# Two-layer decoder trunk on one core: expert rows gathered and results added by indirect transfers instead of one-hot products

## The reference, cut to what matters

```python
def moe_swiglu(h, w_router, wg, wu, wd):          # h = rms_norm(x, norm_ffn)
    logits = (h @ w_router).astype(jnp.float32)
    top_v, top_i = lax.top_k(logits, TOP_K)
    gate = jax.nn.softmax(top_v, axis=-1)
    comb = jnp.sum(jax.nn.one_hot(top_i, N_EXPERTS, dtype=jnp.float32) * gate[..., None], axis=-2)
    out = jnp.zeros_like(h)
    for e in range(N_EXPERTS):
        out = out + comb[..., e:e + 1].astype(h.dtype) * swiglu(h, wg[e], wu[e], wd[e])
    return out                                    # x = x + out; then rms_norm(x, norm_final)
```

## Time and profile before

| | us |
|---|---|
| median of 3 runs | 1719.57 (1717.74 to 1722.81) |
| profiled execution, its own time | 1716.31 |
| its span, first to last instruction | 1714.5 |
| PE busy, share of the span | 1655.3, 97% |
| DVE busy, share | 1229.0, 72% |
| ACT busy, share | 1007.0, 59% |
| HBM read | 457.94 MB, 268 GB/s over the span |
| granted clock of TensorE, mean | 0.991 |

### The profile page before, as it was taken

The page is one execution under the profiler, slowest core; times in us unless marked ns, Lnnn a source line. Parts: engine busy times, 40 slices in busy tenths (PEclk is TensorE's granted clock), DMA queues, the critical chain, the costliest instruction groups (busy, mean ns, idle before and its releaser), DMA issues.

```text
span 1714.5 us, 22148 instructions
## 1 busy us (share of the span) xinstructions
PE 1655.3 (97%) x9025; PEld 1405.8 (82%) x9025; DVE 1229.0 (72%) x879; ACT 1007.0 (59%) x835; POOL 17.3 (1%) x26
## 2 busy tenths in 40 slices
PE   7889999999998999899999999999999999999997
PEld 7769889999876987788878888888888788888885
DVE  5646555444664645888888888888888888888884
ACT  6544343434454434576766767667766677667662
POOL 0000000000000001000000000000000000000000
PEclk9989999999999999899999999999999999999999
DMA  8514425555451345699999999999999998999981
GB/s 312 197 50 160 158 84 206 188 188 199 171 206 50 148 148 197 222 368 362 341 348 356 354 356 344 350 362 346 366 353 351 347 361 341 354 367 346 362 338 73
DMA packets 36327, 459.78 MB, mean 268 GB/s; under 512 B 4144, under 2 KB 4400, under 8 KB 6448
## 3 DMA queue, kind: packets, MB, share of 16 engines
q1 hardware_dynamic: 35424, 455.52, 70.5%
q0 software_dynamic: 848, 3.48, 0.6%
HBM read 457.94 MB, written 1.05 MB: 268 GB/s over the span
## 4 chain that ended last, share of the span: by engine, by line
issue 59%; PE 32%; DVE 4%; ACT 3%; DMA 1%; SPq 0%; POOL 0%; DVEq 0%; ACTq 0%; POOLq 0%
PE PS L734 9%; PE PS L736 9%; PE PS L735 9%; DMA stage<-wl_dram 1%; DVE wlo L1263 1%; ACT probs L418 1%; PE PS L1027 1%; PE PS L999 1%; ACT whi L379 1%; PE PS L740 1%; PE PS L771 1%; PE PS L798 1%; PE PS L817 0%; DVE loA L1281 0%; DVE probs L1306 0%
## 5 line engine op out<-in xcount | busy, mean ns | idle before, releaser
L1263 DVE TENSOR_TENSOR wlo<-stage,whi 128x4096 fp32r<-128x4096 f32 (+2 forms) x226 | 926.4, 4100 | 287.3 <-ACT whi L379 286.1
L379 ACT ACTIVATE whi<-stage 128x4096 fp32r<-128x4096 f32 (+2 forms) x227 | 765.1, 3372 | 366.4 <-DMA stage<-wm_dram 231.3
L734 PE MATMUL PS<-whi,e_hi 128*128 128x512 f32 x896 | 357.1, 399 | 5.7 <-DVE wlo L1263 2.8
L736 PE MATMUL PS<-whi,e_lo 128*128 128x512 f32 x896 | 351.7, 392 | 0.0
L735 PE MATMUL PS<-wlo,e_hi 128*128 128x512 f32 x896 | 350.8, 392 | 0.0
L734 PEld LDWEIGHTS PS<-whi,e_hi 128*128 128x128 f32 x896 | 169.5, 189 | 40.3 <-DVE wlo L1263 3.8
L736 PEld LDWEIGHTS PS<-whi,e_lo 128*128 128x128 f32 x896 | 169.2, 189 | 36.1
L735 PEld LDWEIGHTS PS<-wlo,e_hi 128*128 128x128 f32 x896 | 169.6, 189 | 33.3
L734 PE MATMUL PS<-whi,a_hi 128*128 128x512 f32 x448 | 176.2, 393 | 3.4 <-DVE a_lo L1772 2.4
L735 PE MATMUL PS<-wlo,a_hi 128*128 128x512 f32 x448 | 174.7, 390 | 0.0
L736 PE MATMUL PS<-whi,a_lo 128*128 128x512 f32 x448 | 174.6, 390 | 0.0
(11 more groups left out here) (296 smaller groups left out, 1849.7 us busy)
## 6 DMA issues: line engine op xcount, KB each, us to landing
stage<-wm_dram SPq DMA_DIRECT2D x167, 2048.0 KB, 9.4
stage<-wl_dram SPq DMA_DIRECT2D x20, 2048.0 KB, 8.0
stage<-wf_dram SPq DMA_DIRECT2D x33, 1024.0 KB, 4.8
stage<-wl_dram SPq DMA_DIRECT2D x7, 1816.0 KB, 8.8
w1k<-wl_dram SPq DMA_DIRECT2D x2, 2048.0 KB, 7.7
w1v<-wl_dram SPq DMA_DIRECT2D x2, 2048.0 KB, 12.1
xs<-mem_dram POOLq DMA_DIRECT2D x2, 1024.0 KB, 7.9
stage<-wm_dram SPq DMA_DIRECT2D x2, 1024.0 KB, 6.0
```

Of the source, the lines that this page charges most:

```text
L379: nc.scalar.activation(whi[slot][:, 0:n], stage[slot][:, 0:n], ACT.Copy).then_inc(w_hi[slot], 1)
L734: mm(out, ah, bh, start=start, stop=False)
L736: return mm(out, al, bh, start=False, stop=stop)
L1263: V.tensor_tensor(wlo[slot][:, 0:n], stage[slot][:, 0:n], f32(whi[slot][:, 0:n]), ALU.subtract).then_inc(w_lo[slot], 1)
```

## The change

- **Rows in.** POOL writes x once to an HBM tensor `x_rows` (and a second copy to `sums`). For each item from the second on, POOL gathers the 128 rows of the slots from `x_rows` into `xg` by an indirect DMA (`take`), and PE turns them by 8 transposes (`turn_rows`) into the banks in which the gather's products were before. The first item is still gathered by products (`gather`), now from the unscaled x.
- **Norm factor.** x is gathered without its norm factor. The factor of each slot (`rstd_slot`) is the scale of silu (on the gate product) and a scalar operand of the product of silu and up.
- **Slot facts.** One pair of small products per item (`info`) gives row number, whether the slot is used, norm factor and weight of each slot, from `info_tok`. DVE makes of them the row to take and the row to add to (an unused slot adds to a spare row behind the 256).
- **Rows out.** ACT scales the item's sum and writes it in float32 (`rows_of`); there is no split, no scatter product and no scatter add. POOL adds the rows to `sums` in HBM by an indirect DMA with accumulation (`put`).
- **Last item.** It is scattered on chip as before; its one-hot matrix is made and turned again behind the loop. Before that POOL has loaded x back from `sums`.

```diff
@@ gpsimd, behind the layers
+            pool.wait_ge(x_half, 8)
+            pool.dma_start(x_rows.rearrange("(t p) d -> p t d", p=P), x[:]).then_inc(rows_out, 16)
+            pool.dma_start(sums[0:SEQ, :].rearrange("(t p) d -> p t d", p=P), x[:]).then_inc(put_done, 16)
+            def take(it):
+                pool.drain()
+                pool.wait_ge(take_ready, it)
...
+                    pool.wait_ge(gath_done, it * 2)
+                nc.gpsimd.tensor_tensor(pool_step[:], stat[:, 2:3], stat[:, 3:4], ALU.mult)
+                pool.indirect_dma_start(out=xg[:], out_offset=None, in_=x_rows, in_offset=bass.IndirectOffsetOnAxis(ap=take_next[:], axis=0)) \
+                    .then_inc(xg_in, 16)
+            def put(it):
+                pool.drain()
+                pool.wait_ge(dn_ready, it)
+                pool.wait_ge(put_ready, it)
+                pool.wait_ge(put_done, it * 16)
+                nc.gpsimd.tensor_tensor(pool_step[:], stat[:, 2:3], stat[:, 3:4], ALU.mult)
+                pool.indirect_dma_start(out=sums, out_offset=bass.IndirectOffsetOnAxis(ap=put_now[:], axis=0), in_=down_rows[:], in_offset=None,
+                                        compute_op=ALU.add).then_inc(put_done, 16)
+            take(1)
...
+            with pool.Fori(1, n_items) as it:
+                put(it)
+                take(it + 1)
+            pool.drain()
+            pool.wait_ge(put_done, n_items * 16)
+            nc.gpsimd.tensor_tensor(pool_step[:], stat[:, 2:3], stat[:, 3:4], ALU.mult)
+            pool.dma_start(x[:], sums[0:SEQ, :].rearrange("(t p) d -> p t d", p=P)).then_inc(x_back, 16)
@@ scalar
-                act.wait_ge(f_rstd, NT + t + 1)
-                nc.scalar.activation(xs_hi[:, t, :], x[:, t, :], ACT.Copy, scale=stat[:, 6 + t:7 + t]).then_inc(xg_hi, 1)
+                act.wait_ge(x_half, 4 + 2 * t + 2)
+                nc.scalar.activation(xs_hi[:, t, :], x[:, t, :], ACT.Copy).then_inc(xg_hi, 1)
+            def rows_of(it):
+                act.wait_ge(put_ready, it)
+                act.wait_ge(put_done, it * 16)
+                nc.scalar.activation(down_rows[:].rearrange("p (b n) -> p b n", b=2), PS[:, 2:4, :], ACT.Copy, scale=gate_slot).then_inc(dn_ready, 1)
-                        down_parts()
+                        rows_of(it)
-                    nc.scalar.activation(hid_tok[:, 0, :], bank(0), ACT.Silu).then_inc(m_silu, 1)
+                    if s == 0:
+                        act.wait_ge(slot_ready, it + 1)
+                    nc.scalar.activation(hid_tok[:, 0, :], bank(0), ACT.Silu, scale=rstd_slot).then_inc(m_silu, 1)
-                    if s == 5:
-                        act.wait_ge(ohT_done, it + 1)
-                        nc.scalar.activation(gate_slot, bank(6)[:, SEQ:SEQ + 1], ACT.Copy)
-                        nc.scalar.activation(onehot_T[:], bank(6)[:, 0:SEQ], ACT.Copy).then_inc(ohT_ready, 1)
@@ tensor
+            def info(cols):
+                for t in range(NT):
+                    ins = mm(bank(5)[:, cols], f32(onehot[:, t, :]), info_tok[:, t, cols], start=(t == 0), stop=(t == NT - 1))
+                ins.then_inc(info_done, 1)
+            def turn_rows(it):
+                pe.wait_ge(xg_in, it * 16)
+                for k in range(KD):
+                    ins = nc.tensor.transpose(bank(6 + k // 4)[:, (k % 4) * P:(k % 4) * P + P], xg[:, k * P:(k + 1) * P], ident)
+                    if k % 4 == 3:
+                        ins.then_inc(gath_done, 1)
-                        pe.wait_ge(ohT_ready, it + 1)
-                        gather(it + 1)
+                        turn_rows(it + 1)
-                            pe.wait_ge(md_lo, it)
+                            pe.wait_ge(dn_ready, it)
-                    if 1 <= s <= 4 and not first:
-                        scatter(it, s - 1)
-                    if s == 4:
...
+                    if s == 3:
+                        pe.wait_ge(oh_ready, it + 2)
+                        info(slice(0, 4))
@@ vector
-                V.tensor_tensor(hid_tok[:, 1, :], hid_tok[:, 0, :], bank(1), ALU.mult).then_inc(m_mul, 1)
+                V.scalar_tensor_tensor(out=hid_tok[:, 1, :], in0=bank(1), scalar=rstd_slot, in1=hid_tok[:, 0, :],
+                                       op0=ALU.mult, op1=ALU.mult).then_inc(m_mul, 1)
-                    if s == 1 and not first:
-                        down_parts(it)
-                    if 2 <= s <= 5 and not first:
-                        scatter_add(it, s - 2)
+                    if s == 2:
+                        if not first:
+                            dve.wait_ge(put_done, it * 16 + 16)
+                            V.tensor_copy(put_now[:], put_next[:])
+                            V.tensor_copy(gate_slot, info_next[:, 3:4]).then_inc(put_ready, 1)
+                        dve.wait_ge(info_done, it + 2)
+                        onehots(it + 1)
+                        gate_of(it + 1, oh_ready)
+                    if s == 4:
+                        dve.wait_ge(info_done, it + 3)
+                        V.tensor_copy(info_next[:], bank(5)[:, 0:4]).then_inc(row_done, 1)
...
+                        V.tensor_copy(take_next[:], info_next[:, 0:1]).then_inc(take_ready, 1)
```

More of the change, by code:

```diff
@@ L721, in _ @@
                     nc.scalar.activation(a_hi[:], bank(4), ACT.Copy).then_inc(ma_hi, 1)
+            act.wait_ge(ohT_done, 1)
+            nc.scalar.activation(onehot_T[:], bank(5)[:, 0:SEQ], ACT.Copy).then_inc(ohT_ready, 1)
             act.wait_ge(w_used[2], n_items * MOE_STEPS + MOE_USED[2])
+            act.wait_ge(put_ready, n_items)
+            act.wait_ge(put_done, n_items * 16)
             down_parts()
@@ L1211, in item @@
                     if s == MOE_STEPS - 1:
-                        pe.wait_ge(ohT_ready, it + 1)
-                        gather(it + 1)
+                        turn_rows(it + 1)
                     if not begin:
                         if s == 1 and not first:
-                            pe.wait_ge(md_lo, it)
+                            pe.wait_ge(dn_ready, it)
                         down_e(n, s == 1, s == 0)
-                    if 1 <= s <= 4 and not first:
-                        scatter(it, s - 1)
-                    if s == 4:
[L1221 to L1226, removed]
+                    if first and s == 1:
+                        pe.wait_ge(gt_ready, 1)
+                        info(slice(3, 4))
+                    if s == 3:
+                        pe.wait_ge(oh_ready, it + 2)
+                        info(slice(0, 4))
             pe.wait_ge(xg_lo, 2)
             gather(0)
+            pe.wait_ge(info_ready, 1)
+            info(slice(0, 3))
             item(0, first=True)
@@ L1236, in _ @@
             turn(steps)
+            pe.wait_ge(oh_last, 1)
+            for t in range(NT):
+                ins = nc.tensor.transpose(bank(5)[:, t * P:(t + 1) * P], f32(onehot[:, t, :]), ident)
+            ins.then_inc(ohT_done, 1)
             keep_busy(7, 40)
@@ L1697, in onehots, with slots_of, gate_of @@
                     ins = V.tensor_scalar(onehot[:, t, :], cst("iota", 0, CAP), 1.0, keys[:, t, bass.ds(it, 1)], ALU.add, ALU.is_equal)
-                ins.then_inc(oh_ready, 1)
-            def gate_of(it):
-                V.tensor_copy(gate_tok, combs[:, :, bass.ds(it, 1)].rearrange("p t o -> p (t o)")).then_inc(gt_ready, 1)
+                return ins
+            n_row = [0]
+            def slots_of():
+                V.scalar_tensor_tensor(out=row_f[:], in0=info_next[:, 1:2], scalar=spare_neg, in1=info_next[:, 0:1], op0=ALU.mult, op1=ALU.add) \
+                    .then_inc(row_done, 1)
+            def gate_of(it, ready=None):
+                V.tensor_copy(info_tok[:, :, 3:4], combs[:, :, bass.ds(it, 1)]).then_inc(ready or gt_ready, 1)
             def mlo(kind, n):
@@ L1727, in _ @@
             gathered_lo(0)
+            dve.wait_ge(info_done, 1)
+            V.tensor_copy(rstd_slot, bank(5)[:, 2:3]).then_inc(slot_ready, 1)
+            V.tensor_copy(info_next[:, 0:3], bank(5)[:, 0:3]).then_inc(row_done, 1)
+            dve.wait_ge(row_done, 1)
+            slots_of()
+            dve.wait_ge(row_done, 2)
+            V.tensor_scalar(put_now[:], row_f[:], spare, None, ALU.add)
             mlo(0, 1)
```

89 lines of the change are left out of this document (57 added, 32 removed).

## The result

The changed kernel takes 1729.74 us (median of 20 runs, 1721.65 to 1744.04), the kernel before 1722.47 us (20 runs, 1713.84 to 1728.59). The ratio is **1.0048, interval 1.0034 to 1.0063**: slower by some 8 us (6 to 11 by the interval), where 9.0 were forecast. So the two traces are 18.6 us apart where the medians are 7.3 apart. Counts, shapes and the kind of waits can be compared between them; a difference of one or two us per item can't.

What follows compares the result with a forecast made beforehand. PE and the buffers' ring were taken to bind together. PE in items -8, end -2.7, DMA +19.2 and start +0.5 sum to +9.0 us, from 1719.57 to 1728.6 us; likeliest case 1722 to 1738, full range 1707 to 1752.

Steps and rivals of the forecast that it cites:

- Both loops bind together: Expert stage: PE has work for 99.6% of an item, and the buffers' ring runs flat out for 98.8%.
- Forecast A: Expert stage: ring bound, half of the new DMA time reaches it, 1722 to 1738 us; chance 0.40.
- 0.2 us per step: Expert stage: the time a buffer's ring waits for PE, 17.6 us ring against 17.8 step; some 1.5 us per item.
- The term -8 us for PE in the items: Seven items: the ring gives back 1.2 us each of what it waits for PE; bounds 0 and -11 us.
- I take 1.2 us for the items: Per item: two thirds or more of the ring's 1.5 us wait for PE, as some slots are late for DMA.
- the end's 2.7: Last item: its uncovered 3.5 us gather for an item that doesn't exist becomes 0.8 us, saving 2.7 us.
- The term +19.2 us for DMA: Expert stage: half of 38.3 us new engine time, from gathers, scatters and x coming back, reaches the ring.
- Rival C: Expert stage: transfers fall into gaps and the freed ring gives all it waits for, -10.7 us, 1709 us; chance 0.27.
- Rival B: Expert stage: a quarter of the DMA time arrives and cancels the gain, -0.6 us, 1719 us; chance 0.15.
- Rival D: DMA engines: their added time counts in full, cancelling the PE gain in part, +31.6 us, 1751 us; chance 0.10.
- Rival E: DVE's wait at step 2: scatter later than 25.3 us; at 30 us, +33 us on A, 1761 us; chance 0.08.
- Signs named in advance: Expert stage: PE busy 94 to 96%, wlo waits 4 us or more per item, landing about 9.8, share 0.95, items 125 to 127.

Runs made afterwards that it cites:

- halved kernel before: Kernel before with each expert load, high half and low half done in two halves of 2048 columns under own semaphores: 1702.83 us, ratio 0.9927.
- without row transfers: Changed kernel with gathers from the third item on and the seven accumulating scatters replaced by 8 KB transfers under the same waits: 1711.97 us, ratio 0.9972.
- put-back run: Changed kernel with 20 useless PE products of 512 columns added per item, 4.5 us per item: 1725.00 us, ratio 1.0050 to the kernel before.
- trace with plain scatters: Changed kernel with the scatters as plain writes, without accumulation: 1715.45 us, ratio 1.0010 to the kernel before.
- halved changed kernel: Changed kernel with each expert load, high half and low half done in two halves of 2048 columns under own semaphores: 1670.52 us, ratio 0.9728.

## Why the prediction was right, and where its terms were not

**The bound: right.** "Both loops bind together" is what the experiments show from both sides. PE's 4.7 us per item are worth 0.3 +- 4 us in all while the ring is as it was, and 32 us once it is shorter. The row transfers cost 13 us with the long ring, and 0.7 +- 5 with the short one. Forecast A (the ring bound, part of the new DMA time reaches it) is what happened, at 8 us against 9.0.

**The slack of the ring.** The text found that PE stood idle for 0.5 us per item, from the busy column (2.97 us in 780). The halved kernel before has an item of 123.73 us against 124.69, so about 0.96 us per item were to be had. The busy column covers short stalls, because ends of products are modelled and overlap what follows. The items one by one show how the two loops bind together: three of the seven items of before take 123.71 us, PE's own pace, and the others up to 126.87, so that now PE sets the pace and now the ring. The ring's slack was read rightly. From each load's issue and landing and its two halves (125 loads, 860 to 1600 us) the mean ring of before is 9.29 landing + 0.21 until ACT starts + 3.64 + 0.09 + 4.42 + 0.16 until the next issue = 17.81 us, and the 0.21 is the "0.2 us per step" of the text, though this came from a median landing of 9.5 and left the small gaps out.

Halving the loads gave before 12.5 us and not the 2 to 5 expected. In the traces 6.8 us of it lie in the seven items and 4.1 in the item ahead of them. A further 5.3 us of the traces' difference are not the edit's: they stand ahead of the expert stage, in code that is the same.

```profile
677.00 0.56 POOL L375 TENSOR_TENSOR stat<-stat 128x1 f32<-128x1 f32 x1 [8.84 <-DVE stat L1573]
```

This is the power of the earlier trace rows, at 682.31 us there.

**The term -8 us for PE in the items: too large.** The step that failed is "I take 1.2 us for the items (two thirds or more of the 1.5, as some ring slots are late for the DMA anyway)". With the end's 2.7 it made -10.7. Putting the work back gives 0.3 +- 4 us for both, leaving the row transfers out gives 4.8 +- 3.5 us for both and all the rest. The end's 2.7 us are seen in the timeline, so the items' part is at most 1.4 us by the first and at most 5.6 by the second, and not 8. What stood in its place: the time that a landed buffer waits for ACT did fall, from 0.21 to 0.05 us per load, 1.1 us per item, which is the step's 1.2. But it did not come out as a shorter ring: the mean ring is 18.02 us without row transfers and 18.24 with them, as the landing grew. How much of this growth is the change's and how much belongs to these two slow executions one trace each can't tell, and why the freed time was not given back stays open. That loads bunch up once PE no longer spaces them is a guess for which the traces show little: the times between issues scatter by 0.93 us before and by 0.99 without row transfers.

**The term +19.2 us for DMA: too large as well.** 17.6 of it, half of 35.2 us, were for gathers and scatters; 13 +- 4 us were measured, and with PE's work put back 8.6 +- 2.8 for this, x coming back and the start together, where 19.7 were put down. Engine time per item was 4.0 us, not 4.8: a gather 1.4 (1.6 taken), an adding scatter 2.7 (3.2 taken). By these sizes half of it, for the seven gathers and seven scatters that the experiment replaced, is 7 x 0.7 + 7 x 1.35 = 14 us, within the first interval; the second is about a quarter. So "half", a choice between the ends, is now bounded for one kernel: a quarter with PE's work in place, half without it. The 3.1 us for x coming back, 1.6 in the sum, weren't tested by themselves.

The two errors have opposite signs and cancel to within 1 us. By the put-back run PE's terms are 0.3 +- 4 us for the -10.7 forecast, and all the others 8.6 +- 2.8 for +19.7; by the run without row transfers the rows are 13 us for +17.6, and all the rest together -4.8. That the total came out within 1 us is luck; that it is positive and small follows from the bound.

**Rival C (faster)** put 1709 us and is refuted by the time. Its own test, landings at 9.5 us, does not decide, since landings of 9.5 stand in the trace with plain scatters, whose runs (1.0010) are no faster than before either. It would have needed the freed ring to give all it waited for. **Rival B** (a quarter of the DMA time arrives) had the share right by the put-back run, but PE's -10.7 with it, which did not come.

**Rival D (every byte costs)** put 1751 us and doesn't fit the halved changed kernel either. That kernel moves 379 GB/s at a DMA share of 0.99, against 354 GB/s in the changed kernel. So the engines' and the memory's limit lay above what the ring asked for, and the ring's length set the pace. The Trainium skill, DMA: Bandwidth & Descriptors, section on bandwidth, gives the 358 GB/s as each core's part when both cores of an HBM domain stream, and up to 425 GB/s for one core alone, on 16 MB. Here one core is at work, and this trace agrees: 379 GB/s were held for 740 us. So the price of 1737 in the prediction set two cores' share against one core's stream.

**Rival E (the scatter is late)** had 11 us to spare. The timeline of ACT, POOL and DVE for one scatter, and its landing:

```profile
1599.89 1.10 ACT L717 ACTIVATE down_rows<-PS,stat 128x1024 f32<-128x1024 f32 x1
1600.02 4.42 DVE L1322 TENSOR_TENSOR wlo<-stage,whi 128x4096 fp32r<-128x4096 f32 x1 [3.02 <-ACT whi L428]
1601.15 3.34 POOL L404 TENSOR_TENSOR pool_step<-stat 128x1 f32<-128x1 f32 x1 [60.09 <-ACT down_rows L717]
1604.65 1.60 POOL L405 DMA_INDIRECT sums<-down_rows,put_now  x1 [0.15 <-issue]
...
1627.91 0.68 DVE L1855 TENSOR_TENSOR a_lo<-PS,a_hi 128x512 fp32r<-128x512 f32 x1
1628.52 0.15 DVE L1886 COPY put_now<-put_next 128x1 int32<-128x1 int32 x1
```

```profile
DMA to landing us min/median/max: 12.8/12.8/12.8
```

The rows are ready at 1601.0, POOL's step ends at 1604.5, the scatter lands at 1604.65 + 12.8 = 1617.5, and DVE comes to its wait after 1628.5 without idle time: 16.5 us of the cover of 27.5 are used, where some 20 were put down. The landing took 12.8 us and not 8, but only one slow POOL step lay in the way instead of two. From 860 to 1640 us no wait of DVE for this transfer is listed.

**Signs named in advance.** PE busy fell to 95.7% of the stage (94 to 96). The waits for the low half alone are 2.9 us per item, under the 4 named; with those for `a_lo` and `e_lo` they are 5.2. The DMA share is 0.94 and not 0.95, landing 9.9. The item of the profiled execution, 127.36 us, is just above "125 to 127"; that execution is 5.2 us above its median, 0.7 us per item. A single profiled execution differs from the median of its kernel by as much as the whole effect (-7.0 to +5.2 us here), so signs of one us per item need the ratio beside them.

## What to carry to other kernels

When a ring of buffers and an engine are both full, taking work from the engine may be worth next to nothing until the ring is shorter, as here. Add up the ring of one buffer (landing, and each pass over it, to the next load) and compare it with the step, before valuing any saving; here 17.6 us stood against a step of 17.8 before the change, and 9.9 + 3.6 + 4.4 = 17.9 against 18.2 after it. A ring is shortened without moving fewer bytes by refilling the buffer in halves with semaphores of their own: that alone gave 12 us, made the change worth 32, and the two together are 2.7% faster than the kernel before.

## What the runs showed of the hardware

- An adding scatter of 128 rows of 4 KB took 2.7 us of all 16 engines, a plain one and a gather about 1.3 to 1.4. From issue to landing, beside a full stream of loads, the adding scatter took 13.8 and the gather 10.3 us (medians), where a load of 512 KB on nearly idle engines took 3.9.
- A load of 1 MB lands in 7.4 us while the engines are 0.99 busy, one of 2 MB in 9.9 us. Halving the size saves a quarter of the landing. By these rows the ring of one half is some 7.4 + 1.9 + 2.3 = 11.6 us (an estimate, without its waits) for 17.9 with the whole; 2.5 us of the difference are the landing's and 3.8 the two passes', as one half is split while the other lands. The halves also raised the traffic from 354 to 379 GB/s with the same bytes per item.
- A POOL operation on one column took 3.34 us in the timeline above, where it began inside a low half of DVE and ended with it (1604.49 and 1604.44), and 0.19 us when DVE had just gone idle (its last operation ended at 1152.21):

```profile
1152.37 0.19 POOL L395 TENSOR_TENSOR pool_step<-stat 128x1 f32<-128x1 f32 x1 [60.49 <-DVE take_next L1898]
```

  Seventeen times the duration costs nothing here, as 11 us of cover are left, but it stands ahead of each transfer that POOL issues. The Trainium skill, SBUF — State Buffer, section on who interferes with whom, says that a DVE instruction with two SBUF inputs and a GpSimd instruction that reads SBUF exclude each other for a whole instruction; these two rows agree.
- The mean landing of the same 2 MB loads was 9.29 to 9.79 us in seven traces, in nearly the order in which the executions were fast or slow for their kernel. What lengthens it from one execution to the next stays open; a third of a microsecond in a single pair of traces isn't an effect of an edit.
- Ahead of the expert stage, in the same code, two executions were 5.3 us apart (677.00 and 682.31 us). A difference of two whole traces is to be taken apart by stages before it is put down to an edit.
